# Conditioning pieces loaded one weight load earlier, fewer of them in the down projections, and the low parts of the down weights made on VectorE

## The reference

```
ada = silu(c) @ w_ada[l] + b_ada[l]            # nine vectors of 1024: shift, scale, gate for three steps
x += 0.5 * gate1 * SwiGLU1(modulate(rmsnorm(x)))   # u @ w_up (1024 x 5632), silu(a)*b, @ w_down (2816 x 1024)
x += gate2 * mix(modulate(rmsnorm(x)))             # u @ w_in, window attention with sinks and RoPE, pooling, w_out
x += 0.5 * gate3 * SwiGLU2(modulate(rmsnorm(x)))
```

## Time and profile before

| | us |
|---|---|
| median of 3 runs (lowest, highest) | 2016.4 (2015.2, 2019.59) |
| the profiled execution, its own time | 2017.73 |
| its span, first to last instruction | 2015.6 |
| busy in it: PE, PEld | 1960.3, 1755.6 |
| busy in it: DVE, ACT, POOL | 1463.1, 854.4, 271.7 |
| moved by DMA | 265.25 MB, mean 132 GB/s |

### The profile page before, as it was taken

One profiled execution on the slowest core, in us unless ns is written; L12 is line 12 of the kernel. 1 busy time (PEld: TensorE's weight loads), 2 busy tenths in 40 slices (PEclk: granted clock), 3 DMA queues, 4 the chain that ended last, 5 costly groups with the idle time before them and its releaser, 6 DMA issues.

```text
span 2015.6 us, 32068 instructions
## 1 busy us (share of the span) xinstructions
PE 1960.3 (97%) x12511; PEld 1755.6 (87%) x12511; DVE 1463.1 (73%) x2245; ACT 854.4 (42%) x1502; POOL 271.7 (13%) x172
## 2 busy tenths in 40 slices
PE   9999999999989999999999999999999999999999
PEld 7889989887778989998888999898777789899998
DVE  4896877876776868769686976966767758558572
ACT  3443535333513535335453534453343235344351
POOL 1212021201000020211201021120100000210202
PEclk9999999999999999999999999999999999999999
DMA  9454453535444344544343543533545433333332
GB/s 301 149 167 154 118 169 100 135 118 165 136 127 155 85 156 116 162 131 117 126 129 119 152 156 104 159 125 64 166 132 156 130 100 95 96 95 108 105 108 79
DMA packets 344934, 265.25 MB, mean 132 GB/s; under 512 B 50318, under 2 KB 326978, under 8 KB 344784
## 3 DMA queue, kind: packets, MB, share of 16 engines
q1 hardware_dynamic: 342960, 262.63, 43.1%
q10 hardware_dynamic: 1536, 0.46, 0.1%
q0 software_dynamic: 288, 0.11, 0.0%
HBM read 261.07 MB, written 2.10 MB: 131 GB/s over the span
## 4 chain that ended last, share of the span: by engine, by line
PE 84%; DVE 8%; ACT 3%; issue 3%; DMA 2%; SPq 1%; ACTq 0%; DVEq 0%
PE bank L2354 11%; PE bank L2356 11%; PE bank L2355 11%; PE bank L2195 10%; PE bank L2197 9%; PE bank L2196 9%; PE ps L2195 4%; PE ps L2196 4%; PE ps L2197 4%; DVE ada_acc L1552 2%; PE bank L2279 2%; PE bank L2280 1%; PE bank L2283 1%; PE ps L2356 1%; PE ps L2355 1%
## 5 line engine op out<-in xcount | busy, mean ns | idle before, releaser
L930 POOL TENSOR_TENSOR w_lo<-stage,w_hi 128x640 fp32r<-128x640 f32 (+2 forms) x130 | 244.3, 1895 | 1559.5 <-ACT w_hi L993 1521.0
L2354 PE MATMUL bank<-u_hi,w_hi 128*128 128x256 f32 x1136 | 322.8, 284 | 11.9 <-ACT w_hi L1009 11.3
L2355 PE MATMUL bank<-u_lo,w_hi 128*128 128x256 f32 x1136 | 322.1, 284 | 0.0
L993 ACT ACTIVATE w_hi<-stage 128x640 fp32r<-128x640 f32 (+3 forms) x257 | 217.4, 865 | 153.1 <-DMA stage<-in_w_pool_o 63.8
L2195 PE MATMUL bank<-u_hi,w_hi 128*128 128x512 f32 x632 | 252.5, 400 | 0.3 <-DVE prod L1655 0.3
L2197 PE MATMUL bank<-u_hi,w_lo 128*128 128x512 f32 x632 | 246.4, 390 | 0.0
L2196 PE MATMUL bank<-u_lo,w_hi 128*128 128x512 f32 x632 | 246.2, 390 | 0.0
L2356 PE MATMUL bank<-u_hi,w_lo 128*128 128x256 f32 x852 | 241.7, 284 | 0.0
L2354 PEld LDWEIGHTS bank<-u_hi,w_hi 128*128 128x128 f32 x1136 | 218.4, 192 | 16.2 <-ACT w_hi L1009 13.8
L2355 PEld LDWEIGHTS bank<-u_lo,w_hi 128*128 128x128 f32 x1136 | 218.6, 192 | 0.8
L1009 ACT ACTIVATE w_hi<-stage 128x512 fp32r<-128x512 f32 (+1 forms) x213 | 160.0, 768 | 130.4 <-PE bank L2356 42.0
(11 more groups left out here) (289 smaller groups left out, 4424.1 us busy)
## 6 DMA issues: line engine op xcount, KB each, us to landing
stage<-in_w_ff_up SPq DMA_DIRECT2D x172, 512.0 KB
ada_stage<-in_w_ada SPq DMA_DIRECT2D x80, 512.0 KB, 6.1
ada_stage_mix<-in_w_ada SPq DMA_DIRECT2D x48, 512.0 KB, 4.8
stage<-in_w_ff_down SPq DMA_DIRECT2D x24, 960.0 KB
stage<-in_w_in SPq DMA_DIRECT2D x16, 1024.0 KB
stage<-in_w_ff_down SPq DMA_DIRECT2D x16, 896.0 KB
ada_block<-in_w_ada SPq DMA_DIRECT2D x8, 1024.0 KB, 11.9
stage<-in_w_out SPq DMA_DIRECT2D x8, 1024.0 KB
```

The source lines that it names most:

```text
L930: nc.gpsimd.tensor_tensor(raw_tile(w_lo, e, key), raw_tile(stage, e, key), hi_tile(e, key), ALU.subtract).then_inc(lo_ready, 1)
L993: nc.scalar.activation(hi_tile(e, key), raw_tile(stage, e, key), ACT.Copy).then_inc(hi_ready, 1)
L2354: mm(dst, hi[:, k, :], r_hi_[:, k, :], start=(k == 0 and w in (1, 7)), stop=False, skip_group_check=True)
L2355: mm(dst, hi[:, k, :], r_lo_[:, k, :], start=False, stop=False, skip_group_check=True)
```

## The change

It does five things.

1. SP issues each piece one weight load earlier: `n - 1` in place of `n` in both functions, so the piece stands ahead of the load behind which it stood.
2. Other points. Mixing (e = 1, 4): one piece at each of tiles 6 to 25 and two each at tiles 42 and 43, in place of one at 6 to 21 and two each at 22 to 25. Feed-forward e = 2, 3: at the ends of runs 0 to 3 now 2, 3, 2, 2 (before 3, 1, 3, 3), in the ways down 3, 2, 3, 7 (before 4, 4, 3, 3). Event 0 keeps 3 at each run's end and 4, 4, 4, 5 in the ways down, a few at an earlier m.
3. The low parts of all down tiles move from POOL to DVE: D(p,0) and D(p,1) at the end of the run's last pair, ahead of the pieces there, and D(p,m+2) at the head of step m.
4. The loads of positions and sinks are issued on POOL's queue, behind its two low parts of event 0 and the wait for `t_lo_ready` 4, in place of ACT's queue.
5. DVE's eight angle steps stand at the end of pair 10 of event 0. The sines and `angles_done` come one way down earlier and in the last at m = 2. ACT's `root_ready` stands at m = 1 in every event.

In the order of the file (the points, SP, GpSimd, ScalarE's `down`, VectorE's `pair` and `down`):

```diff
     if e % 3 == 1:
-        return [("M", n) for n in (*range(6, 22), 22, 22, 23, 23, 24, 24, 25, 25)]
+        return [("M", n) for n in (*range(6, 26), 42, 42, 43, 43)]
     if e == 0:
...
-                + last_of(2, 3) + down(2, 0, 1, 1, 2) + last_of(3, 3) + down(3, 1, 2, 2, 3, 3))
+                + last_of(2, 3) + down(2, 0, 0, 1, 2) + last_of(3, 3) + down(3, 0, 1, 2, 3, 3))
     if e in (2, 3):
-        return (last_of(0, 3) + down(0, 0, 1, 2, 3) + last_of(1, 1) + down(1, 0, 1, 2, 3) + last_of(2, 3) + down(2, 0, 2, 3)
-                + last_of(3, 3) + down(3, 1, 2, 3))
+        return (last_of(0, 2) + down(0, 0, 1, 2) + last_of(1, 3) + down(1, 1, 2) + last_of(2, 2) + down(2, 0, 1, 2)
+                + last_of(3, 2) + down(3, 0, 1, 1, 2, 2, 3, 3))
...
-                return next((n for n in range(len(FF_ITEMS)) if slot_free(e, n) >= taken), len(FF_ITEMS) - 1)
+                return next((n - 1 for n in range(1, len(FF_ITEMS)) if slot_free(e, n) >= taken), len(FF_ITEMS) - 1)
...
-                return next((n for n in range(len(MIX_LOADS)) if mix_slot_free(e, n) >= taken), len(MIX_LOADS) - 1)
+                return next((n - 1 for n in range(1, len(MIX_LOADS)) if mix_slot_free(e, n) >= taken), len(MIX_LOADS) - 1)
...
             pool.wait_ge(lo_ready, START_TILES)
+            for n in range(START_TILES, DVE_TILES):
+                low_part(0, ("U", n))
+            positions_load()
             for l in range(DEPTH):
-                ff(event(l, 0))
...
-                ff(event(l, 2))
...
-                    if e == 0 and p == 1 and m == 2:
-                        positions_load()
-                    if e == 0 and final and m == 3:
+                    if e == 0 and p == 2 and m == 3:
                         act.wait_ge(setup_step, DEPTH + 8)
...
+                if last:
+                    low_part(e, ("D", p, 0))
+                    low_part(e, ("D", p, 1))
                 pieces(e, (j, 0))
+                if e == 0 and j == RUN_ENDS[1]:
+                    for n in range(8):
+                        angle_step(n)
...
+                    if m + 2 < KT:
+                        low_part(e, ("D", p, m + 2))
                     if not final and m == 1:
                         gate_sum(e, end)
...
                     if ahead and m == KT - 3:
-                        dve.wait_ge(lo_ready, lo_done(e, ("D", p, KT - 1)))
                         low_part(e + 1, first_tile(e + 1, 0))
...
-                    if e == 0 and final and m < 2:
-                        for step in range(4 * m, 4 * m + 4):
-                            angle_step(step)
-                    if e == 0 and final and m == 5:
+                    if e == 0 and final and m == 2:
                         angles_done()
```

More of the change, by code:

```diff
@@ L931, in low_part, with positions_load @@
                                         ALU.subtract).then_inc(lo_ready, 1)
[L933 to L941, removed]
+            def positions_load():
+                pool.wait_ge(t_lo_ready, 4)
+                pool.dma_start(pos_i[:, :], positions[0].partition_broadcast(P)).then_inc(late_in, 16)
+                with nc.allow_non_contiguous_dma(reason="eight sinks"):
+                    for i in range(DEPTH):
+                        for t in range(2):
+                            pool.dma_start(sink_all[t * CHUNK:(t + 1) * CHUNK, i, :],
+                                          sinks[i].rearrange("(b t) -> t b", t=2)[t].partition_broadcast(CHUNK)
+                                          ).then_inc(late_in, 16)
             def window_sums(l, g):
@@ L1195, in down @@
                     if final and after:
-                        if m == (1 if e else 4):
+                        if m == 1:
                             root_ready(e + 1)
@@ L1205, in ff @@
                     down(e, p, run[-1])
[L1207 to L1211, removed]
-                        for t in range(2):
-                            act.dma_start(sink_all[t * CHUNK:(t + 1) * CHUNK, i, :],
-                                          sinks[i].rearrange("(b t) -> t b", t=2)[t].partition_broadcast(CHUNK)
-                                          ).then_inc(late_in, 16)
             def attend(l, a):
```

## The result

The changed kernel takes 2043.1 us (median of 3 runs, 2041.2 to 2045.4), the kernel before 2016.4: 1.3% slower (ratio 1.013, 95% interval 1.0105 to 1.0154). The forecast was 2000.2, that is faster. The medians differ by 26.7 us. The two profiled executions, from which all rows are read, differ by 23.4 us (spans of 2015.6 and 2039.0), so 23.4 us are to be found in them.

The account below looks back on a forecast made before the run. PE, busy 97% of the span, bounds the kernel, so only its waits and the clock lost behind them can be won. Gains of 6.5, 3.1, 1.3, 3.3 and 2.0 sum to 16.2 us: median 2000.2 us, range 1987 to 2014.

Parts of the forecast that it names:

- event 0: First feed-forward event: 5 us gained in ways down p = 0 to 2, 0.5 and 1.0 in the last: 6.5 us.
- events 2, 3: Feed-forward events: PE's waits at p = 0 to 2 go (3.9 plus 1.5 clock; 3.4), p = 3 loses 2.3 and 2.1.
- mixings: Events 1 and 4: waits and clock of 6.0 + 2.3 and 4.7 + 2.3 become 4 + 1: gain 3.3 and 2.0.
- SP's order: Pieces sent a load earlier: DVE finds them there, but mixing loads for tiles 26 to 31 go later; 4 us wait, 1 clock.
- The prediction's own sign: Mixings: the forecast is wrong if PE's wait at tiles 28 to 30 is 8 us or more, or gone.
- Rival C: SP's queue: weights wait behind pieces, +18 us in the mixings and +8 in the ways down: 2026; chance 0.14.
- Rival C's other half: Ways down: load of pair end+1 stands behind the piece at D(p,2), some 1 us at each of eight places, +8.
- The positions: Event 0: POOL issues position and sink loads at about 90 us, pieces due at 98: cost 0, bounds -2 and +4.
- Rival D: Event 0: positions landing over 85 us after issue stop DVE and PE; at 100 us, 2015 in all; chance 0.04.
- The step at D(3,0): Events 2 and 3, p = 3: PE's wait for `h_lo` of 1.4 us grows to 3.4; 2.3 and 2.1 us lost.
- The low parts: Ways down: subtractions moved from POOL add 114 us on DVE; 14.5 us come back as pieces get shorter.
- The mixings' new points: Four pieces at tiles 42 and 43 (5.1 us and 5.4 of sums) meet tiles of 5.45 us, three ahead of PE: hidden.

Follow-up runs that it names:

- e1: The changed kernel, except that in the mixings GpSimd's queue issues the pieces, so no weight load in SP's queue stands behind one: 1995.7 us.
- a1: The changed kernel with one line taken back: in the mixings a piece is issued behind the same load as in the kernel before: 2011.5 us.
- e4: The kernel before with one line changed: in the feed-forward blocks a piece is issued one load earlier: 2004.2 us.
- b1: a1 with the four sink transfers issued by GpSimd at about 56 us, ahead of the first pieces: 2005.2 us.
- d2: b1 with the mixings' last four pieces at tiles 38 to 41 and the old points of use in events 0, 2 and 3: 1987.1 us.
- d1: b1 with the mixings' last four pieces at tiles 38 to 41 and feed-forward pieces behind the same load as in the kernel before: 2010.6 us.
- d4: The kernel before with one part of the change alone, the low parts of the ways down on VectorE: 2026.7 us.
- b5: b1, but GpSimd again makes the low parts of the ways down, as in the kernel before: 2002.6 us.
- e3: d3, but GpSimd makes the low parts of the ways down: 1989.3 us.
- b2: b1 with the old points of use in the mixings: 2005.8 us.
- f1: d3 with the mixings' last pieces at tiles 42, 42, 43, 43 and the mixings' pieces on GpSimd's queue as in e1: 1985.7 us.
- d3: b1 with mixings' last four pieces at tiles 38 to 41; in events 2, 3 the sixteenth piece at the third way down's fourth tile: 1986.4 us.

## Why the prediction was wrong

| term | forecast | measured |
|---|---|---|
| event 0 | +6.5 | +2.4 |
| events 2, 3 | +3.1, +1.3 | +1.9, +2.1 |
| mixings | +3.3, +2.0 | -15.2, -14.6 |
| sum | +16.2 | -23.4 |

**The step that failed** is "SP's order": "The load of tiles 28 and 29 stands behind piece 21, which waits for that: about 571.8, not 567.4", and the load after it "at 580, not 572.9", from which came 4 us of wait and 1 of clock. They went at 587.6 and 596.8. The walk was right in kind and began too late. It took the load of tiles 26 and 27 as the first that a piece holds up (562.3 us; it went at 577.2). In the new order it happens at each load from 452 us on: a later load makes DVE's low part later, DVE then takes the piece behind that low part later, and that piece holds up the next load. The loop runs over twelve loads (those issued from 452.00 to 596.84) and was priced for three. In event 1 PE then waited 7.9 us for low parts and 9.0 in attention and pooling (before 6.0 and 2.8), and lost 6.9 us more to the lower clock. Measured, the loop costs 23 and 21 us a mixing (after against e1); going back to the old place gives 18 and 15 of it (a1). The prediction's own sign, a wait of 8 us or more at tiles 28 to 30, did not show: it was 5.4 and 0.7 us there. It looked at the end of the loop alone.

Rival C was this mechanism, at 0.14, priced 18 us above the forecast for the mixings, where 35.1 came (5.3 forecast and 29.8 lost). Its condition, "a landing of about 6 us after issue", was the wrong one: from issue to ACT's rounding it was 5.7 us for the load at 577.16 and 6.3 for that at 587.57, and waits began at 460. What decides is whether the piece's wait is met before or after the load's own slot is free. The code compares the two as counts of PE's tiles, as if DVE took a piece when PE ends the tile. But in the kernel before DVE had taken the pieces of tiles 6 to 25 only 3 to 11 us after PE's end of their tile: the load of tiles 26 and 27 went at 556.54, when PE ended tile 22, and DVE was done with that tile's first piece at 561.9. This lag could be read at every load, and the prediction used it at three. Rival C's other half, 8 us in the ways down, did not come: there the same early order gave 6.5 and 5.1 us (e4).

**The positions** were put at 0, with +4 as the upper bound, taken from ACT's 4 us of issues and SP's issue of 8.22 us. The sinks cost a wait of 10 us there, and event 0 as a whole 7.5 (398.8 in a1, 391.3 in b1); without the collision it gains 9.4 where 6.5 was forecast. The bound was wrong since the rows told what an issuing queue loses, not what a transfer beside it loses (12.6 us to land), and since nothing was asked about who stands behind that piece. The trace of the kernel before had that price too: with the sinks on ACT's queue from 192.3 us on, SP's pieces of 190.66, 193.49 and 200.62 landed after 10.3, 10.1 and 12.6 us, the longest of all:

```profile
DMA to landing us min/median/max: 3.5/6.1/12.6
```

So it is not GpSimd's queue that makes the sinks slow for others; ACT's did the same. Rival D looked at the positions' own lateness, which never mattered: their landing took 4.4 us. The rule weighed there (the Trainium skill, SBUF — State Buffer, section "SBUF: two separate sides", a lock-out of GpSimd's descriptors by VectorE) has no effect that can be seen here. With VectorE at work GpSimd's issues took 0.59 us, four in 2.48 us, and in e1 0.53 us each, 48 times; those pieces landed in 3.9 us (median), SP's in 3.5. Whether VectorE's instructions were of the kind the rule means, no run shows.

**Events 2 and 3** came within 1.2 us of their terms, which is less than profiles of the same code differ, so the agreement may be luck. The step at D(3,0) came nearly to the digit: PE waited 3.1 us for `h_lo`, forecast 3.4; the waits of p = 2 went. But the parts were read wrongly. The gain was put to the balance of the windows under the new points; e4 and d2 show that the order alone gives more (353.4 and 354.4 against 358.0) and that beside it the new points take a part back. Where the order is old they do help (d1 against d4).

**The low parts** were priced right in DVE's time and taken as neutral for PE. They are neutral only beside early pieces (b5, e3); alone they cost 10 us (d4). What comes back was too small: DVE's busy time rose by 54.5 us (60 to 80 forecast), so 57 of the 111.8 came back. The prediction's working had 14.5 of that, the shorter pieces alone; its sign of 60 to 80 allowed for more without a working.

**The mixings' new points.** The prediction called the pieces at tiles 42 and 43 hidden. In after and e1 they are: PE has no wait there. They show, with 3.6 us a mixing, only where the old order sends the last piece late (a1, b1). With the old order the new points win nothing that can be told (b1 against b2).

## What to carry to other kernels

A queue that waits before an issue is a resource like an engine: list for each entry what it waits for and when that comes, and move nothing that waits for a late consumer ahead of a load that feeds the same consumer, since that closes a loop in which every late load makes the next one late. Such a loop is priced over all its turns, or broken by giving one of the two streams its own queue. And a transfer of tiny elements goes where nothing awaits a DMA: four of them took the traffic beside them to about a quarter for ten microseconds, cost PE 10 us when issued at 91 us and 9 at 376, and nothing to be seen at 56.

## What was not expected of the hardware

Four transfers of the sinks, a few KB in all, held a transfer of 512 KB, issued 1 us after the last of them on another queue, for 12.6 us and took the core's traffic from 237 to 64 GB/s over 10 us, at a DMA share of 0.55. And TensorE's granted clock fell to a mean of 0.55 from 110 to 120 us, behind a wait of 10 us, where in b1, with a wait of 2.2 us, it was 0.87; 1.00 is 2.4 GHz, 0.50 is 1.2 (third column from the right; after first, then b1):

```profile
110.00:120.00 10.00, 4.01 (x11) 3.23 (x12) 9.64 (x23) 1.89 (x3) 0.00 (x0) 0.55 0.44 145
```

```profile
110.00:120.00 10.00, 10.00 (x40) 8.10 (x40) 7.14 (x10) 3.48 (x5) 0.00 (x0) 0.87 0.73 210
```

GpSimd's queue, which issued a 512 KB transfer in 0.53 us, was as good for the pieces as SP's: f1 and d3 are not told apart.
